# First mixer of a two-layer diffusion backbone: the last query slab split around the first scores, tile 3's taps in two sums, the rotation inside PSUM, and the softmax diagonal in the form that also sums

## The reference

```python
px = xm @ w_in; ph = hm @ w_in                 # 512 q, 128 k, 128 v, 1024 conv inputs per token
qx = apply_rope(q of px); kx = apply_rope(k of px)   # latent tokens only; context carries no position
ax = window_gqa(qx, kx, vx, kh, vh, sink, scale)     # 8 heads, 2 kv heads, one softmax with a sink logit
bx = conformer_conv(px[..., i_u:], w_dw, b_dw, ln_g, ln_b)
#   y = a * sigmoid(g); depthwise convolution, 31 taps, + b_dw; silu(layer_norm(y))
ox = concatenate([ax, bx]) @ w_out
```

## Time and profile before

| | us |
|---|---|
| median of 3 runs | 1801.29 (1800.66 to 1802.83) |
| the profiled execution | 1797.72 |
| its span | 1795.9 |

### The profile page before, as it was taken

How to read it: one execution, slowest core, us unless ns; L and a number is a source line. 1 busy time by engine, 2 the same in 40 slices (tenths; PEclk the granted TensorE clock), 3 DMA queues, 4 the chain that set the end, 5 groups by cost and what they waited for, 6 DMA issues and landing times.

```text
span 1795.9 us, 24360 instructions
## 1 busy us (share of the span) xinstructions
PE 1693.7 (94%) x9054; PEld 1441.7 (80%) x9054; DVE 1169.1 (65%) x1981; ACT 611.5 (34%) x828; POOL 133.5 (7%) x70
## 2 busy tenths in 40 slices
PE   7999999999958899999999999999999889989996
PEld 1888888888847698888888888888888866879996
DVE  3777777777887768777777763553333875555555
ACT  2321222234446443212312332222223444344434
POOL 2000000002855000000000000000000131000000
PEclk9999999999966999999999999999999989989999
DMA  8454555532210015455555323432223221134543
GB/s 341 165 198 176 199 195 187 214 131 81 94 47 1 1 48 199 189 186 214 198 184 199 129 95 117 147 111 93 95 101 109 95 70 48 48 126 179 184 169 116
DMA packets 45718, 245.93 MB, mean 137 GB/s; under 512 B 5200, under 2 KB 6352, under 8 KB 25424
## 3 DMA queue, kind: packets, MB, share of 16 engines
q1 hardware_dynamic: 45648, 244.98, 37.3%
HBM read 243.91 MB, written 1.05 MB: 136 GB/s over the span
## 4 chain that ended last, share of the span: by engine, by line
PE 81%; DVE 12%; ACT 3%; issue 3%; DMA 1%; POOL 0%; ACTq 0%; DVEq 0%; SPq 0%; POOLq 0%
PE ps L1376 14%; PE ps L1378 14%; PE ps L1385 14%; PE ps L1224 11%; PE ps L1225 10%; PE ps L1226 10%; PE ps L1250 4%; PE ps L1447 2%; ACT w_hi L550 1%; DVE w_lo L937 1%; DVE rt L808 1%; DVE work L840 1%; DVE ps L1046 1%; DVE a_lo L848 1%; DVE ss L788 1%
## 5 line engine op out<-in xcount | busy, mean ns | idle before, releaser
L937 DVE TENSOR_TENSOR w_lo<-raw,w_hi 128x2048 fp32r<-128x2048 f32 x142 | 325.1, 2292 | 327.8 <-ACT w_hi L550 288.0
L1376 PE MATMUL ps<-a_hi,w_hi 128*128 128x512 f32 (+1 forms) x1280 | 453.1, 364 | 8.3 <-DVE work L957 8.3
L1378 PE MATMUL ps<-a_lo,w_hi 128*128 128x512 f32 (+1 forms) x1280 | 452.5, 363 | 0.0
L550 ACT ACTIVATE w_hi<-raw 128x2048 fp32r<-128x2048 f32 x88 | 168.6, 1916 | 370.7 <-PE ps L1385 347.4
L1376 PEld LDWEIGHTS ps<-a_hi,w_hi 128*128 128x128 f32 x1280 | 242.7, 190 | 46.8 <-DVE work L957 8.0
L1224 PE MATMUL ps<-h_hi,w_lo 128*128 128x512 f32 (+1 forms) x776 | 269.6, 347 | 7.5 <-DVE h_lo L964 6.3
L1378 PEld LDWEIGHTS ps<-a_lo,w_hi 128*128 128x128 f32 x1280 | 242.7, 190 | 37.3
L1385 PE MATMUL ps<-a_hi,w_lo 128*128 128x512 f32 (+1 forms) x1280 | 269.0, 362 | 0.0
L1225 PE MATMUL ps<-h_lo,w_hi 128*128 128x512 f32 (+1 forms) x776 | 267.9, 345 | 0.0
L1226 PE MATMUL ps<-h_hi,w_hi 128*128 128x512 f32 (+1 forms) x776 | 267.9, 345 | 0.0
L1385 PEld LDWEIGHTS ps<-a_hi,w_lo 128*128 128x128 f32 x1280 | 220.0, 189 | 37.4
(11 more groups left out here) (194 smaller groups left out, 2022.4 us busy)
## 6 DMA issues: line engine op xcount, KB each, us to landing
raw<-wstream SPq DMA_DIRECT2D x157, 1024.0 KB, 4.9
mring<-wmod SPq DMA_DIRECT2D x144, 512.0 KB, 3.6
xT<-tokens SPq DMA_DIRECT2D x4, 512.0 KB, 6.9
cb<-cond SPq DMA_DIRECT2D x1, 1024.0 KB, 7.6
out<-spare SPq DMA_DIRECT2D x8, 128.0 KB, 1.9
cst<-consts SPq DMA_DIRECT2D x1, 448.0 KB, 7.7
vec<-vecs SPq DMA_DIRECT2D x1, 174.0 KB, 8.1
ccol<-cond_cols SPq DMA_DIRECT2D x1, 8.0 KB, 1.6
```

The lines of the kernel that those rows point to most:

```text
L550: act.activation(w_hi[:, (w + j) % 2], raw[:, (w + j) % 2], ACT.Copy).then_inc(hi_ready, 1)
L937: dve.tensor_tensor(w_lo[:, slot], raw[:, slot], w_hi[:, slot].bitcast(F32), ALU.subtract).then_inc(lo_ready, 1)
L1376: pe.matmul(bank, hi, a_hi[:, k, 0:nt], start=k == 0, stop=False, skip_group_check=True)
L1378: pe.matmul(bank, hi, a_lo[:, k, 0:nt], start=False, stop=False, skip_group_check=True)
```

## The change

- **Slab split.** Slab 5 is done one query tile after the other, each with its own signal. Of slab 6 only query tile 2 (piece 4) is done before the attention; tile 3 (piece 5) goes to bank 3 in TensorE's iteration 2, behind unit 2's scores. Pieces 4 and 5 are rotated and rounded in units 3 to 5 instead of 0 and 1. Before unit 1's scores TensorE now waits for the whole convolution of tiles 0 and 2 (`conv_op`), since these end later than before.
- **Taps.** ScalarE writes a first product for tile 3 as well (tap 12) and GpSimd sums its taps in `conv[:, 3]` without waiting for VectorE; VectorE keeps its 12 taps in bank 2, one in each of units 0 to 11, and one more addition joins the two sums before the layer norm. GpSimd's additions fall from 49 to 48, of which 23 instead of 20 have their products ahead of the attention; its low part of slab 8 moves behind its 29th addition.
- **Rotation.** In this mixer the shuffled latent half and its product with the cosines stay in the piece's PSUM bank; the second mixer keeps the old form.
- **Pieces.** ScalarE copies the context half of K ahead of its wait for slab 4, and VectorE puts one tap between each rotation and its subtraction.
- **Diagonal.** The multiplication by the identity has an accumulating output added (`accum_out`), in both mixers; the sums are not used.

The core of the diff follows; the three versions of `ab_beside` in it are ScalarE's, VectorE's and TensorE's, in this order.

```diff
+        CONV_ADDS = 2 * TAPS - 2 - OWN_TAPS
+        ADDS_AFTER = (0, 0, 4, 8, 12, 16, 20)
+        ADDS_EARLY = 23
+        ADDS_AHEAD = ADDS_EARLY + 6
+        TAPS_AFTER = (0, 5, 21, 36, 43)
+        TAPS_PIECE = ((1, 9), (1, 4), (1, 3), (1, 1))
...
+            return sq[:, 1] if j == N_AB - 1 else full[:, ROPE_INDEX[j] % 2]
...
                     if n == TAPS - 1:
-                        pool.wait_ge(conv_op, CONV_OPS)
+                        pool.wait_ge(tap_first, 2)
...
-            for c in range(7):
+            for c in range(6):
                 split_lo(W_AB + 2 + c, (W_AB + c) % 2)
                 add_taps(ADDS_AFTER[c], ADDS_AFTER[c + 1])
-            add_taps(ADDS_AFTER[7], CONV_ADDS)
+            add_taps(ADDS_AFTER[6], ADDS_AHEAD)
+            split_lo(W_AB + 8, (W_AB + 6) % 2)
+            add_taps(ADDS_AHEAD, CONV_ADDS)
...
+            context_copy(0, AB_PIECES[0])
+            act.wait_ge(slab_done, w + 5)
+            split_hi(w + 6, w % 2, w + 6)
+            act.wait_ge(glu_done, 3)
+            act.activation(v_rows, ps[1][:], ACT.Copy).then_inc(v_copy, 1)
+            rounded_piece(0, AB_PIECES[0])
+            first_product(3, OWN_TAPS)
+            tap_products(ADDS_AFTER[4], ADDS_AFTER[5])
+            context_copy(1, AB_PIECES[1])
+            rounded_piece(1, AB_PIECES[1])
+            act.wait_ge(slab_done, w + 6)
+            split_hi(w + 7, (w + 1) % 2, w + 7)
+            context_copy(2, AB_PIECES[2])
+            tap_products(ADDS_AFTER[5], ADDS_AFTER[6])
+            rounded_piece(2, AB_PIECES[2])
+            pieces(3, AB_PIECES[3])
+            tap_products(ADDS_AFTER[6], ADDS_EARLY)
 
             def ab_beside(i):
...
+                if i in (3, 4):
+                    context_copy(i + 1, AB_PIECES[i + 1])
+                if i in (4, 5):
+                    rounded_piece(i, AB_PIECES[i])
+                if i == 3:
+                    act.wait_ge(slab_done, w + 7)
                     split_hi(w + 8, (w + 6) % 2, w + 8)
...
+            def rotate_in_bank(src, dst):
+                sw, t = src[:, LAT:TOK], sq[:, 0, 0:LAT]
+                link(dve.stream_shuffle(sw, src[:, 0:LAT], [(i + 16) % 32 for i in range(32)]))
+                link(dve.tensor_tensor(t, sw, sin, ALU.mult))
+                link(dve.tensor_tensor(sw, src[:, 0:LAT], cos, ALU.mult))
+                return dve.tensor_tensor(dst, sw, t, ALU.add)
...
                         for n in range(len(qts)):
                             last = dve.tensor_scalar(rdiag[:, e % 2, n], ident, rinv[:, at + n:at + n + 1], None,
-                                                     ALU.mult)
+                                                     ALU.mult, ALU.add, accum_out=rsum[:, e % 2, n:n + 1])
...
+            for j, (between, after) in enumerate(TAPS_PIECE):
+                if AB_PIECES[j][3]:
+                    rotated_piece(j, AB_PIECES[j])
+                    even_odd_taps(at, at + between)
+                    low_piece(j, AB_PIECES[j])
+                else:
+                    even_odd_taps(at, at + between)
+                    pieces(j, AB_PIECES[j])
+                even_odd_taps(at + between, at + between + after)
+                at += between + after
 
             def ab_beside(i):
...
+                if i in (4, 5):
+                    low_piece(i, AB_PIECES[i])
+                if i in (3, 4):
+                    rotated_piece(i + 1, AB_PIECES[i + 1])
+                last_tile_taps(min(i, OWN_TAPS), min(i + 1, OWN_TAPS))
                 if i == LN_UNIT:
                     dve.wait_ge(conv_op, CONV_OPS)
                     dve.wait_ge(tap_add, CONV_ADDS)
+                    link(dve.tensor_tensor(conv[:, 3], ps[LN_BANK][:], conv[:, 3], ALU.add))
...
-            two_tiles((w + 5) % 2, (2, 3), TOK).then_inc(slab_done, 1)
+            one_tile((w + 5) % 2, 0, 2).then_inc(step_done, 1)
+            one_tile((w + 5) % 2, 1, 3).then_inc(slab_done, 1)
...
-            two_tiles((w + 6) % 2, (0, 7), TOK).then_inc(slab_done, 1)
+            one_tile((w + 6) % 2, 0, 0).then_inc(step_done, 1)
             pe.wait_ge(piece_lo, 3)
...
             def ab_beside(i):
 
+                if i == 0:
+                    pe.wait_ge(conv_op, 2 * (TAPS + 1))
                 if i == 2:
                     pe.wait_ge(piece_lo, AB_EARLY)
-                if i == 3:
+                    one_tile((w + 6) % 2, 1, 3).then_inc(slab_done, 1)
+                if i == 5:
+                    pe.wait_ge(piece_lo, 5)
+                if i == 7:
                     pe.wait_ge(piece_lo, N_AB)
```

88 lines of the change are left out of this document (42 added, 46 removed).

## The result

| | before | after |
|---|---|---|
| median, five runs side by side | 1801.29 (1799.63 to 1805.51) | 1790.70 (1790.05 to 1792.21) |
| ratio | | 0.9934, 95% interval 0.9921 to 0.9947 |
| profiled execution, its span, mean clock | 1797.72, 1795.9, 0.968 | 1790.70, 1788.9, 0.975 |
| busy TensorE, VectorE in us | 1693.7, 1169.1 | 1684.9, 1165.4 |

The change gained 10.6 us; I had forecast 5.3. The forecast's path through the mixer can be laid beside the trace. The start of the program moves by some microseconds from one execution to the next, so I count from VectorE's second evaluation of the gated unit (the sigmoid product that feeds the convolution, one per channel tile): 445.24 in the trace before, 447.25 after. The end is ScalarE's table load behind the attention (628.50 before, 621.29 after).

The account below looks back on a forecast made before the run. The prediction took the kernel as bound by matmuls except where VectorE holds them up. Gains of 2.0 to unit 6, 2.0 and 2.5, less 1.2, made 5.3 us: 1796.0 on the median, own range 1791 to 1801, whole range 1788 to 1804.

Parts of the forecast that it names:

- To the first scores: Before the first mixer's attention: first scores at 502.5 instead of 506.83 us, 4.3 gained, 2.5 left at unit 0's maxima.
- K's moved stall: Before the first scores: K's subtraction, with two SBUF inputs, waits for GpSimd's slab from 480, taking some 4 us.
- Units 0 to 3: First mixer: moved slab half takes 7.9 us, half at each clock; unit 3's maxima at 520.4 instead of 528.55, 8.1 gained.
- Units 3 to 6: First mixer: part is given back; unit 6 19.5 us behind 521.2, at 540.7 instead of 542.75, 2.0 gained.
- the stall of unit 4's scaling: In units 3 to 6: unit 4's two-column scaling waits on VectorE beside GpSimd's work on slab 8, 2.7 us.
- Units 6 to 12: First mixer: ScalarE's 5.5 us stall goes; three pairs of units at 8.0 make 24.0 instead of 25.96, 2.0 gained.
- Units 12 to 16: First mixer: no GpSimd additions from unit 13, no VectorE taps; two pairs of 8.18 make 16.4 instead of 18.95, 2.5 gained.
- Behind unit 16: End of the first mixer's attention: one more addition, 0.7 us, and slightly longer diagonals, together 1.2 lost.
- The two moved stalls don't happen: K's subtraction or unit 4's scaling arrives clear of GpSimd: 11.5 us gained, 1789.8; chance 0.20.
- The diagonal still waits: The summing diagonal on VectorE still waits for GpSimd as before: 1.3 us gained, 1800.0; chance 0.12.
- Half clock: TensorE stays at 1.2 GHz from unit 2 to unit 12, so the change is slower: 5.1 us lost, 1806.4; chance 0.15.
- rival 1: The case that the two moved stalls of VectorE behind GpSimd don't happen: 1789.8 us; chance 0.20.

Follow-up runs that it names:

- x2_waits: Changed kernel with slab 6's low part on VectorE, tile 1's rounding ahead of the waiting tap product, eight useless matmuls before the second mixer's scores: 1786.19 us, ratio 0.9911.
- a3_clock: Changed kernel with 45 useless TensorE matmuls, 35 ahead of the first scores and 10 behind unit 0's scores: 1787.64 us, ratio 0.9918.
- b2_two_sums: Kernel before with only tile 3's taps in two sums, so GpSimd no longer waits for VectorE's taps: 1794.68 us, ratio 0.9955.
- b3_clock: Kernel before with four useless matmuls in each of units 6 to 15 and nothing of the change: 1801.65 us, ratio 0.9995.
- a1_old_diag: Changed kernel with the diagonal built as before, without the accumulating output: 1796.73 us, ratio 0.9959.

## Why the forecast was right in direction and half the size

- *To the first scores.* Right: 0.8 us too early counted from the second evaluation, 0.5 too late from the third; the difference came in with the half clock at 445 us, which the sum could not know. The clean rotation, K's moved stall (said "some 4 us", 4.21) and the wait of tile 1's rounding all came; x2_waits, which treats two of them, gained 4.7 us there.
- *Units 0 to 3.* Right. "I take half of it at each clock, 7.9 us": nine products at 1.2 GHz, the rest at 2.4, 7.4 us in all. With the clock up (a3_clock) the half took 5.5 us and the stretch was 3.5 us shorter, more than the 1.9 that the slab half alone gave.
- *Units 3 to 6.* Right, 20.2 us for 20.3, with the stall of unit 4's scaling (2.59 for 2.7). Some of this is luck: the terms add up to 19.1 and not to the 19.5 that I wrote, and they start at 521.2 where the stage before had ended at 520.4. By the terms as they stand unit 6 would have been 1.2 us earlier. The measured 1.1 us more than the terms include TensorE's products and scores behind unit 5, 5.21 us at a clock of 0.69.
- *Units 6 to 12.* Right in mechanism: 3.0 us gained for 2.0. b2_two_sums gives 4.0 with the waits removed, b3_clock nothing by the clock.
- *Units 12 to 16.* The step that failed: "two pairs like the one of 8.18 make 16.4". I took that pair's time as what VectorE, ScalarE and TensorE need for their handing over. But TensorE was busy through all of it, at a mean clock of 0.62; the pair of 5.98, which I had put down at 0.91 from a row of 10 us, ran wholly at 1.00:

```profile
579.48:587.66 8.18, 8.18 (x33) 6.40 (x32) 4.52 (x14) 4.04 (x11) 1.27 (x1) 0.62 0.00 0
562.73:568.71 5.98, 5.74 (x40) 4.87 (x41) 5.64 (x16) 4.96 (x16) 3.36 (x3) 1.00 0.01 3
```

Two pairs like the second make 12.0, and 12.05 were measured. I had kept the half clock for a rival that makes it slower, and never asked for the mirrored case, that the change removes half clock which the kernel before paid for. b3_clock shows 4.3 us of the 6.9 by the clock alone, with 16 extra matmuls in the stretch; how the other 2.6 divide between these matmuls and what the change took out there (five of ScalarE's six tap products and six of GpSimd's seven additions), no run separates. Nor does a run say why the clock stays up there in the changed kernel.

- *Behind unit 16.* 2.6 us lost instead of 1.2. The diagonal's form is 0.3 of it (a1_old_diag: 43.2 from unit 16 to the end, the changed kernel 43.5, before 40.8), and b2_two_sums, with the one more addition, takes 0.7 longer than before, as forecast. In units 16 to 20 the clock was 0.83 where it had been 0.90; every version that keeps the change's rotation and reaches unit 16 early takes 19.4 to 19.6 us there. What causes it is not shown.
- *Rivals.* "The two moved stalls don't happen" gave nearly the measured time (1789.8), by a mechanism that did not occur. "The diagonal still waits" did not either, and a1_old_diag shows that it would not have mattered. "Half clock" was the right quantity with the wrong sign. The measured median lies outside the forecast's own range of 1791 to 1801, just above the value of rival 1.
- *From the mixer to the median.* The mixer's end moved by 9.2 us from the second evaluation and by 10.5 from the third, the median by 10.6; the two traced executions lie only 7.0 apart, since the changed kernel's came to the second evaluation 2.0 us later. If the late third evaluation is no doing of the change, the mixer gives the whole of the median's gain. The other candidate is the tail: some of the kernel before's executions may have had the long one. On each of the three chips its executions part at a mean clock of 0.966: those at or below took 1801.89 us or more, and those above it, with one exception, 1802.46 or less, with medians of 1800.3 to 1800.9. That fits, but only one execution of that kernel was traced, and it had the short tail and the early third evaluation; what makes up the last 1.4 us is argued, not shown.

No edit makes the gain alone: in the kernel before, the diagonal's form gives 4.3 us and the two sums 5.0 (6.6 from the third evaluation); taken out of the changed kernel, the form costs nothing and the rotation 5.5 (5.2). So they don't add up. That each is paid out in good part through the clock of units 6 to 16, which can be won only once, fits the clocks in the rows above, but no run shows it. Slab split, the order of the pieces and the late taps were not run by themselves.

## What to carry to other kernels

Before taking a unit's time from a row, read the clock beside it: a stretch at 0.5 to 0.7 is a price that a change may remove as well as add, and the forecast needs both signs. Test it with a few useless matmuls in TensorE's gaps, measured so that they end before the wait does; if the stretch shortens, the clock is a cause; if it doesn't, the clock gave nothing or the fillers took it back, and the waits have to be taken away in a run of their own. And read an edit by milestones inside its own stage, counted from the last one ahead of it, since a stage far away, or one just ahead, can run at another clock from one execution to the next and move the time by more than the edit.
